# A context norm taken into the last feed-forward stage, and one weight remainder moved behind each norm, in a two-block transformer kernel

## The reference, cut to what matters

```
h = layer_norm(concat(meta, x))
for l in range(2):
    h = layer_norm(ALPHA*h + 0.5*swiglu_ffn(h, ffn1_w13[l], ffn1_w2[l]))
    h = layer_norm(ALPHA*h + token_mix(h, w_in[l], ...))
    h = layer_norm(ALPHA*h + 0.5*swiglu_ffn(h, ffn2_w13[l], ffn2_w2[l]))
x = h[:, N_META:]
# second block, even layer: latent x and context ctx, each
#   modulate(rms_norm(., g), shift, scale) @ ev_w_in, then attention and an mLSTM
```

## Time and profile before

| | |
|---|---|
| median of three runs | 2239.87 us |
| the profiled execution | 2244.98 us, of it a span of 2242.8 us |
| TensorE matmul | busy 2169.1 us (97%), 14854 matmuls |
| VectorE | busy 1588.8 us (71%) |
| ScalarE | busy 1061.1 us (47%) |
| GpSimd | busy 178.7 us (8%) |
| granted TensorE clock, mean | 0.989 |

### The profile page before, as it was taken

One profiled execution on the slowest core, in us unless ns is written; L12 is line 12 of the kernel. 1 busy time (PEld: TensorE's weight loads), 2 busy tenths in 40 slices (PEclk: granted clock), 3 DMA queues, 4 the chain that ended last, 5 costly groups with the idle time before them and its releaser, 6 DMA issues. The chain is left out here.

```text
span 2242.8 us, 35433 instructions
## 1 busy us (share of the span) xinstructions
PE 2169.1 (97%) x14854; PEld 1987.4 (89%) x14854; DVE 1588.8 (71%) x2416; ACT 1061.1 (47%) x1547; POOL 178.7 (8%) x198
## 2 busy tenths in 40 slices
PE   9999989999999999999999989999999999999997
PEld 8999979999999998999898776898888887589997
DVE  6877988977887897988851676576555336757774
ACT  5433645443543454644551436345445224746663
POOL 2201102201210200200100010000000001000000
PEclk9999999999999999999998999999999999999999
DMA  6665526666566543676330111023222222013552
GB/s 261 235 234 189 214 77 231 240 222 256 199 234 238 197 151 113 263 268 248 121 117 34 57 59 61 20 76 132 94 94 94 96 86 91 29 56 116 186 184 99
DMA packets 48319, 334.88 MB, mean 149 GB/s; under 512 B 5612, under 2 KB 6716, under 8 KB 8864
## 3 DMA queue, kind: packets, MB, share of 16 engines
q1 hardware_dynamic: 38384, 267.47, 33.1%
q0 software_dynamic: 9776, 65.14, 7.6%
HBM read 331.54 MB, written 1.05 MB: 148 GB/s over the span
## 5 line engine op out<-in xcount | busy, mean ns | idle before, releaser
L2010 DVE TENSOR_TENSOR WLO<-RAW,WHI 128x2048 fp32r<-128x2048 f32 x252 | 589.6, 2342 | 237.4 <-ACT WHI L1444 234.4
L461 PE MATMUL PS<-XB,WHI 128*128 128x256 f32 (+1 forms) x3072 | 698.3, 323 | 7.2 <-DVE XB L2377 4.0
L1444 ACT CAST WHI<-RAW 128x2048 fp32r<-128x2048 f32 x252 | 476.5, 1894 | 304.2 <-DMA RAW<-in_dn_c 78.3
L461 PEld LDWEIGHTS PS<-XB,WHI 128*128 128x128 f32 x3072 | 515.0, 191 | 54.3 <-issue 9.9
L461 PE MATMUL PS<-XHI,WHI 128*128 128x272 f32 (+1 forms) x1760 | 505.2, 290 | 11.3 <-ACT XHI L1452 5.1
L461 PE MATMUL PS<-XHI,WLO 128*128 128x272 f32 (+1 forms) x1760 | 500.8, 288 | 0.0
L461 PE MATMUL PS<-XB,WLO 128*128 128x256 f32 (+1 forms) x1536 | 492.5, 321 | 0.0
L461 PE MATMUL PS<-XLO,WHI 128*128 128x272 f32 (+1 forms) x1760 | 481.4, 287 | 0.2 <-DVE XLO L2052 0.2
L461 PEld LDWEIGHTS PS<-XHI,WHI 128*128 128x128 f32 x1760 | 332.2, 189 | 16.5 <-issue 7.3
L461 PEld LDWEIGHTS PS<-XHI,WLO 128*128 128x128 f32 x1760 | 332.2, 189 | 0.0
L461 PEld LDWEIGHTS PS<-XLO,WHI 128*128 128x128 f32 x1760 | 322.9, 189 | 0.9 <-DVE XLO L2052 0.4
(11 more groups left out here) (366 smaller groups left out, 2701.4 us busy)
## 6 DMA issues: line engine op xcount, KB each, us to landing
AW<-in_ada POOLq DMA_DIRECT2D x48, 1024.0 KB, 7.4
RAW<-in_up_c SPq DMA_DIRECT2D x44, 1024.0 KB, 4.9
RAW<-in_up_a SPq DMA_DIRECT2D x42, 1024.0 KB, 5.4
RAW<-in_up_b SPq DMA_DIRECT2D x42, 1024.0 KB, 5.1
RAW<-in_mix SPq DMA_DIRECT2D x30, 1024.0 KB, 4.9
RAW<-in_dn_a SPq DMA_DIRECT2D x22, 1024.0 KB, 5.0
RAW<-in_dn_b SPq DMA_DIRECT2D x22, 1024.0 KB, 5.1
RAW<-in_dn_c SPq DMA_DIRECT2D x22, 1024.0 KB, 4.9
```

What stands on the lines that cost most here:

```text
L461: return pe.matmul(o, w, x, start=first, stop=last)
L1444: act.copy(WHI1[:, s, 0:w], RAW[:, s, 0:w]).then_inc(w1_high, 1)
L2010: v.tensor_tensor(WLO1[:, s, 0:w], RAW[:, s, 0:w], WHI1[:, s, 0:w].bitcast(F32), ALU.subtract)\
```

## The change

1. Behind norms 0 to 4 (and the input's norm) the remainder of the second of the two first units moves from ahead of the norm to behind its last `low_tile` on VectorE. `two_units_first` follows: it takes the second unit's matmuls with the remainder (16 of the 96) out of the walk over the tiles and does them last, behind a wait for that remainder.
2. The first pair of tiles is scaled in two instructions, so that `ln_scaled` counts five per norm.
3. ScalarE's one-element root, with its table load, moves ahead of the last square (in the mixers ahead of a `high`). `keep_busy` is cut from 11 to 8 and, at the input, from 15 to 10.
4. In the last feed-forward stage: the context's squares at steps 9 and 10, their sum on TensorE behind up unit 11, the root at step 13 and the reciprocal at step 15. Their scratch `SQC` moves to the end of area G.
5. Between `take_tiles` and `norm(5)` VectorE does `in_tiles(0, 0)` and `rest(EVEN0 + 2)`, ScalarE `in_hi(0, 0)` and `high(EVEN0 + 2)`. TensorE works the context half of the first two units of `EVEN0` behind `norm_stats`, then waits for the centring, does the third unit's context half, then sums the latent half's squares.

The main programs' calls are moved behind the functions they now need; that changes no order by itself.

```diff
 two_units_first:
-                for z in range(2):
-                    pe.wait_ge(w1_split, n + z + 1)
+                pe.wait_ge(w1_split, n + 1)
+                pe.wait_ge(w1_high, highs[n + 1])
...
-                            mm(pe, PS[:, 2 * z + j, tk], wl, XHI1[:, k, tk], False, False)
+                            if z == 0:
+                                mm(pe, PS[:, j, tk], wl, XHI1[:, k, tk], False, False)
...
+                pe.wait_ge(w1_split, n + 2)
+                for j in range(2):
+                    for k in range(CT):
+                        last = mm(pe, PS[:, 2 + j, tk], block_of(n + 1, j * CT + k)[1], XHI1[:, k, tk], False, k == CT - 1)
+                last.then_inc(unit1_done, 1)
 norm_stats, input_norm, ffn1 (TensorE):
-                    keep_busy(11, 7)
+                    keep_busy(8, 7)
-                keep_busy(15, 7)
+                keep_busy(10, 7)
+                    if i == 3 and f == 11:
+                        in_stat(0, 0, 7)
 even_inputs (TensorE):
-                pe.wait_ge(tile_taken, 8 * 6)
-                in_stat(0, 0, 4)
-                keep_busy(13, 3)
+                half_pair(EVEN0, 0, 0, 0)
+                pe.wait_ge(ln_centred, 4 * 6)
+                half_unit(EVEN0 + 2, 0, 4)
                 in_stat(0, 1, 7)
-                pe.wait_ge(ln_centred, 4 * 6)
-                half_pair(EVEN0, 0, 0, 0)
-                pe.wait_ge(norm_std[0], in_at(0))
                 pe.wait_ge(ln_std, 7)
-                half_unit(EVEN0 + 2, 0, 4)
                 pe.wait_ge(norm_std[1], in_at(0))
                 half_unit(EVEN0 + 3, 0, 6)
 ffn1 (ScalarE):
+                    if i == 3 and step in (9, 10):
+                        act.wait_ge(ctx_loaded, 16)
+                        for c in (2 * step - 18, 2 * step - 17):
+                            act.activation(SQC[:, 2 * c:2 * c + 2, :], X[:, 2 * c:2 * c + 2, 0:CTX], ACT.Square)\
+                                .then_inc(in_sq[0], 1)
+                    if i == 3 and step == 13:
+                        in_root(0, 0, 7)
-                square_tiles(q, SLF, range(4, 8))
+                square_tiles(q, SLF, range(4, 7))
+                act.activation(DUMMY[:, :], EPSH[:, :], ACT.Sqrt)
+                square_tiles(q, SLF, range(7, 8))
+                if q == 5:
+                    in_hi(0, 0)
+                    high(EVEN0 + 2)
                 norm(q)
 even_inputs (ScalarE):
                 in_square(0, 1)
-                in_root(0, 0, 4)
-                in_hi(0, 0)
-                high(EVEN0 + 2)
                 in_root(0, 1, 7)
                 high(EVEN0 + 3)
 input_norm, norm, ffn1 (VectorE):
+                    for k in range(2):
+                        v.tensor_tensor(PL[:, k, tk], PL[:, k, tk], RSTD[:, tk], ALU.mult).then_inc(ln_scaled, 1)
-                for n in range(2):
-                    rest(n)
+                rest(0)
...
+                rest(1)
...
                     low_tile(e, 6)
                     low_tile(e, 7)
+                    last()
+                    if i == 3 and step == 15:
+                        in_recip(0, 0)
-                take_tiles(q, 0.5 / ALPHA, SLF, lambda: None, lambda: rest(u0 + FFN_STEPS + 1))
-                norm(q)
+                second = lambda: rest(u0 + FFN_STEPS + 1)
+                take_tiles(q, 0.5 / ALPHA, SLF, lambda: None, second if q == 5 else lambda: None)
+                if q == 5:
+                    v.wait_ge(ctx_loaded, 16)
+                    in_tiles(0, 0)
+                    rest(EVEN0 + 2)
+                norm(q, second)
 even_inputs (VectorE):
-                in_recip(0, 0)
-                v.wait_ge(ctx_loaded, 16)
-                in_tiles(0, 0)
-                rest(EVEN0 + 2)
+                rest(EVEN0 + 3)
                 in_recip(0, 1)
                 v.wait_ge(ln_out, 8 * 7)
                 in_tiles(0, 1)
-                rest(EVEN0 + 3)
```

More of the change, by code:

```diff
@@ L199, in build @@
         RSC = place("N", "RSC", 7936, [SEQ])
-        SQC = place("N", "SQC", 2 * CT * L1, [CT, SEQ])
+        SQC = place("G", "SQC", (FT + 14) * L1, [CT, SEQ])
         PR = [place("N", f"PR{n}", 512 * n, [L2]) for n in range(2)]
@@ L623, in zero_borders @@
                     pool.memset(c[:, :, :, 0:258:257], 0.0).then_inc(pool2_step, 1)
-            pool.wait_ge(ln_scaled, 4 * 7)
+            pool.wait_ge(ln_scaled, 5 * 7)
             pool.wait_ge(ln_out, 8 * 7)
@@ L714, in two_units_first @@
                             last = mm(pe, PS[:, 2 * z + j, tk], block_of(n + z, j * CT + k)[0], XLO1[:, k, tk], False,
-                                      k == CT - 1)
-                        if k == CT - 1:
+                                      z == 0 and k == CT - 1)
+                        if z == 0 and k == CT - 1:
                             last.then_inc(unit1_done, 1)
+                pe.wait_ge(w1_split, n + 2)
[3 more added lines that the diff above has]
+                last.then_inc(unit1_done, 1)
             def unit_tile(n, j, bank, hi, lo, tk=slice(0, L1)):
@@ L941, in mixer @@
                 norm_stats(q, SLM)
[L943 to L947, removed]
             def split(n):
@@ L1414, in ffn_latent @@
                 post_stat(3, 1, 0)
+            input_norm()
+            for l in range(DEPTH):
+                ffn1(l, 0)
+                mixer(l)
+                ffn1(l, 1)
             even_inputs()
@@ L1448, in norm_out @@
                 for k in range(CT):
-                    if k % 2 == 0:
-                        act.wait_ge(ln_scaled, 4 * e + k // 2 + 1)
+                    if k < 2 or k % 2 == 0:
+                        act.wait_ge(ln_scaled, 5 * e + (k + 1 if k < 2 else k // 2 + 2))
                     if e < 6:
@@ L1479, in norm @@
                 tk = tokens(q)
-                act.activation(DUMMY[:, :], EPSH[:, :], ACT.Sqrt)
                 act.wait_ge(ln_mean, q + 1)
@@ L1632, in mixer @@
                 norm(q)
[L1634 to L1638, removed]
             def rst(z):
@@ L2046, in scale_pair @@
                 tk = tokens(e - 1)
-                v.tensor_tensor(pair(c, tk), pair(c, tk), bc(RSTD[:, tk], 2), ALU.mult).then_inc(ln_scaled, 1)
+                if c == 0:
+                    for k in range(2):
+                        v.tensor_tensor(PL[:, k, tk], PL[:, k, tk], RSTD[:, tk], ALU.mult).then_inc(ln_scaled, 1)
+                else:
+                    v.tensor_tensor(pair(c, tk), pair(c, tk), bc(RSTD[:, tk], 2), ALU.mult).then_inc(ln_scaled, 1)
             def low_tile(e, k):
@@ L2107, in take_tiles, with norm @@
                 second()
-            def norm(q):
+            def norm(q, last=lambda: None):
                 e = q + 1
@@ L2343, in mixer @@
                 rest(u0 + 14)
[L2344 to L2353, removed]
+                take_tiles(q, 1.0 / ALPHA, SLM, lambda: rest(u0 + MIX_UNITS), lambda: None)
+                norm(q, lambda: rest(u0 + MIX_UNITS + 1))
             vs = Steps(v, vec_step)
@@ L2714, in ffn_latent @@
                 post(3, 1)
+            input_norm()
+            v.wait_ge(start_loaded, 16 * N_START)
+            v.wait_ge(start_set, N_SET)
+            for l in range(DEPTH):
+                ffn1(l, 0)
+                mixer(l)
+                ffn1(l, 1)
             even_inputs()
```

## The result

The change costs time: 2249.71 us, median of 11 runs (2245.80 to 2252.05), against 2241.66 (2238.53 to 2244.61) before, in 11 runs beside them. The ratio is 1.0039, 95% interval 1.003 to 1.0047, so 8 us slower by the medians and 8.7 by the ratio, a little over the 0.3% that a measurement here can tell. The forecast was 2246.2, just on the other side of that line. Of the 3.5 us between, 1.8 is the base: three runs had given 2239.87 where eleven give 2241.66.

A forecast was written before the change was run, and what follows sets the result against it. It took TensorE, busy 97%, as the bound, with VectorE bounding the stretch behind norms. Norm starts +4.4, context's sum +3.4 and second block -1.5 made +6.3 us on a 2239.87 median: 2246.2 us, range 2236 to 2253.

The forecast's parts named there:

- Starts and queue behind the norms: At six norm starts, products begin sooner, but GpSimd's additions delay VectorE's remainders and later units: +4.4 us in all.
- The start behind norm 0: Behind norm 0, earlier `VAR` (0.75 us) and split scaling (0.35 us) bring the first product 1.1 us sooner.
- the race: Whether VectorE's moved remainder issues before GpSimd's first addition; if it wins, norms give about -1, total 2240.8; chance 0.18.
- the main case: Behind the norms, GpSimd's first addition issues first and holds the moved remainder; forecast 2246.2 us, chance 0.40.
- no clock risk: Ahead of first products behind norms, 8 filler calls end 0.8 us early against 0.55 before; clock should stay up.
- The sum in the last feed-forward stage: Context's sum of squares there, 16 matmul passes at 0.213 us, on TensorE's path: +3.4 us, lower bound 0.
- the sum is hidden: Rival: up stage of the last feed-forward takes up the context's sum, 3.4 us; total 2242.8; chance 0.12.
- Norm 5 into the second block: First product 13 us sooner, mostly given back in waits and clock falls: -1.5 us, between -3.2 and +0.2.
- the fall behind it: Second block, behind the 4.6 us wait before the fourth unit: the clock falls again, costing 1.7 us.
- the slower case: Rival "slower outright": clock falls behind the centring wait and the input's norm add 3.4 us, 2249.6; chance 0.18 with another case.
- the slower case's own second place: Behind the input's norm: a clock fall there, each fall costing 1.7 us.
- The slower case's first place: Second block, behind the centring wait: a clock fall there, each fall costing 1.7 us.

The follow-up runs named there:

- e1: Kernel before with only the norms' part (moved remainder, split scaling, earlier table load, less filler): 2245.92 us against 2241.86, ratio 1.0021.
- e6: Changed kernel with seven of eight tiles' squares left out of the context's sum, 14 fewer passes: 2247.33 us, ratio 1.0028 to the kernel before.
- e2: Kernel before with only the context's part (context's norm in the last feed-forward stage, second block's start): 2243.93 us, ratio 1.0014 to the kernel before.
- e3: Changed kernel with GpSimd's additions held until the third and fourth units' remainders are through: 2238.75 us, ratio 0.9993 to the kernel before.
- e9: Changed kernel with only the moved remainders put back ahead of the norms, filler still thin: 2246.11 us, ratio 1.0029 to the kernel before.
- e10: Changed kernel with remainders back ahead of the norms and filler back at 11 calls, 15 at the input: 2241.29 us against 2241.74, ratio 1.0004.
- e11: Changed kernel with 10 filler calls, 13 at the input, instead of 8 and 10: 2247.23 us, ratio 1.0035 to the kernel before.
- e5: Changed kernel with ScalarE's high part of the fourth even unit moved ahead of norm 5: 2242.12 us against 2240.92 for the kernel before, ratio 1.0004.
- e7: Changed kernel with late GpSimd additions, early fourth-unit high part, and context squares folded on VectorE to 4 TensorE passes: 2230.36 us, ratio 0.995 to the kernel before.
- e8: As e7, but with the norms' part of the change undone: 2234.68 us, ratio 0.9972 to the kernel before.
- e4: Kernel before with GpSimd's additions held until the third and fourth units' remainders are through: 2238.52 us, ratio 0.9989 to the kernel before.

## Why the forecast was off by little, step by step

**Starts and queue behind the norms: right in kind, a little too dear.** The start behind norm 0 was to come 1.1 us sooner and came 0.97 sooner. GpSimd's first addition was to hold the moved remainder, and did: the race went as in the main case. The third unit was to be 1.1 later and was 0.95 later (norm 0), 1.1 and 0.95 (norm 3), 0.85 and 0.75 (norm 1), 0.8 and 0.68 (norm 4); the fourth unit behind norm 2, 0.85 and 0.67; the input -0.3 and -0.56. The sum is +3.4 for +4.4. The mis-sized term is the addition's, by little: the first one's 1.62 us had been counted whole, and it held VectorE from 236.95 to its end at 238.25, 1.3 us; the other two had 1.15 each, and (10.17 - 3 x 2.25 - 1.3) / 2 leaves 1.06. e1 measured 4.1 to 4.7 for this half, of it 2.7 in the rest. What makes up the difference is clock. This step had said "no clock risk", and e1's trace has a fall at the input (below).

**The sum in the last feed-forward stage: right.** 3.4 us forecast, 3.46 in the traces, and e6 gave back 3.01 for 14 of 16 passes. The rival "the sum is hidden" falls. The root, the table and the reciprocal cost nothing, as said.

**Norm 5 into the second block: the chain right, the clock mis-sized.** The first product was to begin 13 us sooner. Counted from the sums of norm 5 (1098.54 in after, 1093.48 in before, 5.06 later), 1103.03 is 13.1 sooner than 1111.08. The centring's end was to be at 1112.8, with the 5.06 at 1117.86, and is at 1117.87. The fourth unit: 1126.5, with it 1131.6, and it is 1132.11, behind 4.77 us of idleness for 4.6. The step that failed is the fall behind it, set at 1.7 us: the rows show up to 2.8 over work. It is no accident of one execution: 3.4 us of low clock, a part of it over the wait, stand there in all seven traces with the 4.77 us wait (after, e2, e3, e6, e9, e10, e11), and none in e5, e7 and e8, where the wait is 0.61. From the sums to `CB` it is 52.8 us for 53.2, 0.4 gained where 1.5 was forecast, inside the bounds of -3.2 and +0.2. e2's 2.1 to 3.1 (forecast 1.9) says the same.

**The clock: held too cheap, and its whole price stays open.** The forecast held it at +1.7 us in all, the slower case added 3.4, and the table of executions allows up to 6. One place is the fourth unit's, above. The other that repeats is the input's norm, the slower case's own second place. After's trace has no fall there. But e1, e3, e5, e6 and e7, which have the same first products, have 1.7 or 3.4 us of low clock between 20 and 30, and before, e2, e4 and e8, with the old order and 15 calls of filler, have none. Busy time by stretch in e1, then the same stretch in after:

```profile
24.00:26.00 2.00, 2.00 (x11) 0.50 0.96 388
```

```profile
24.00:26.00 2.00, 2.00 (x17) 1.00 0.98 399
```

This fall costs less than its length, since without it TensorE waits for the third unit's remainder (1.10 us in after). From the reciprocal of the input's norm to the next sums it is 39.46 us in e1, with 3.4 us of low clock, against 38.43 in after with none and 38.42 in e6 with 1.7. The slower case's first place, behind the centring, fell in e3 and e8, and not in after, e2 or e11. The 3.4 us behind the fourth unit's wait and 2.3 at the input (the mean of the traces of after, e1, e3, e5, e6 and e7) make 5.7 of the table's 6 us of low clock, but not 5.7 us of time.

Added up from the rows of the traces, the starts (+3.4), the sum (+3.5) and the second block (-0.4) make 6.5 us for the forecast's 6.3. The starts were 1.0 too dear and the fall behind the fourth unit 1.1 too cheap, so these two errors cancelled, and that is luck. Measured are 8.0 to 8.7. Of the 1.5 to 2.2 us between, the input's fall is worth up to 1.0; the other places stay open, as falls come and go between executions: the one trace of after lies in an execution that is 0.8 us below the median, and that of before 3.3 us above its own. The slower case's 2249.6 is the measured time, but it stood on a base 1.8 us too low: as a change it was +9.7, of which 8.0 to 8.7 came. Its reason, low clock on top of the forecast's waits, is half of the truth.

**Base.** The median of three runs was 1.8 us low.

## What to carry over

Before an instruction is moved past a norm, look at what GpSimd does at the new place: the remainder cost 2.3 us where it stood and 3.4 where it went, and moving GpSimd's sums as well turned a loss of 4 to 5 us (e1) into a gain of 4 (e7 against e8). Where TensorE is the bound, give each new wait two prices, its length and the low clock behind it, and check whether filler still reaches the next product when that product moves. But a low stretch that ends in a wait is not to be counted twice. A chain that ends in a wait (root, high part, remainder) is worth reading backwards: the high part needed none of what stood ahead of it, and one moved line was worth 7.8 us.

## What was not expected of the hardware

Whether the clock falls after some 2 us of idleness is not settled by the length of the idle time. TensorE's first products behind such a wait, before, then after, with the granted clock of the stretch behind each:

```profile
497.01 0.48 PE L461 MATMUL PS<-GHI,WHI 128*128 128x272 f32 x1 [1.99 <-DVE SG L2147]
1033.74 0.39 PE L461 MATMUL PS<-GHI,WHI 128*128 128x256 f32 x1 [2.05 <-DVE SG L2147]
...
498.00:500.00 2.00, 2.00 (x10) 0.50 0.00 0
1035.00:1037.00 2.00, 2.00 (x19) 1.00 0.03 8
```

```profile
1037.29 0.39 PE L461 MATMUL PS<-GHI,WHI 128*128 128x256 f32 x1 [2.13 <-DVE SG L2159]
```

1.99 us brought a fall, 2.05 in the same trace did not, 2.13 did, and so did 1.89. Across the other traces the lengths overlap further: in e9 a fall followed 1.36 us and some shorter waits (230.26, above), and in e5 none followed 2.68:

```profile
497.18 0.39 PE L461 MATMUL PS<-GHI,WHI 128*128 128x272 f32 x1 [2.68 <-DVE SG L2159]
...
498.00:500.00 2.00, 2.00 (x18) 1.00 0.00 0
```

Nor is a wait needed. The longest low stretch of every kernel here is 17 to 20 us long and lies in the second block (1182 to 1204 in before). TensorE is busy ahead of it and through it. In before the clock fell some 2 us after narrow matmuls of 16 columns had begun among the others (1180.49), and it rose again at 1203, behind the last of them (1198.10). It is the same in all kernels, so it prices nothing of the change, but it is 8.5 to 10 us of the low-clock column. Before:

```profile
1180.00:1182.00 2.00, 2.00 (x18) 1.00 0.00 0
1184.00:1188.00 4.00, 4.00 (x20) 0.50 0.22 91
```

So one trace can't price such a wait, and a mean over executions can at least bound it: low clock scatters by 2.5 us (one standard deviation of 33 executions) within the kernel before, and lies 10 us higher in e9 than in before. The other surprise was how steady the rest is: 2216.9, 2217.0, 2217.2 and 2217.3 for the kernel before in four groups of 33, 24, 13 and 17 executions, while the medians of these groups lay between 2240.15 and 2241.86.
